# Feed-forward of a two-layer step: the up-projection by seven block products, the down-projection in a stage of its own, GpSimd adding the weight blocks

## The chip, the cores and the metric

One core of a Trainium2 chip. The metric is the device time of one launch in microseconds (us), median of several runs. TensorE (PE; PEld is its weight load), VectorE (DVE), ScalarE (ACT), GpSimd (POOL) and SyncE (SP, which issues the transfers here) each run their own list of instructions in order and wait for each other on semaphores.

## The reference, cut to what matters

A step of a model of two layers over 1088 tokens (1024 of a prompt, 64 of a sample), in float32. Each layer is an attention mixer, its output projection, and a gated feed-forward with a convolution over three tokens:

```python
def conv_ffn(h, buf, w_up, w_conv, b_conv, w_down):
    gate, up = jnp.split(h @ w_up, 2, axis=-1)
    ...
    ext = jnp.concatenate([buf.astype(gate.dtype), gate], axis=1)
    gc = b_conv + ext[:, 0:s_len] * w_conv[0]
    for i in range(1, CONV_W):
        gc = gc + ext[:, i:i + s_len] * w_conv[i]
    y = (jax.nn.silu(gc) * up) @ w_down
    return y, ext[:, ext.shape[1] - (CONV_W - 1):]
```

`h` is 1088 x 1024, `w_up` 1024 x 5632 (2816 gate features, then 2816 up features), `w_down` 2816 x 1024; there is one such pair of matrices for each layer.

## The kernel before

Every large product of float32 is made as three products of rounded parts (`three_passes`): an operand is split into a high part (ACT copies it to the rounded type) and a low part (DVE subtracts that copy from it), and high x high, high x low and low x high are summed in one PSUM bank. Each of the three is a weight load of 128 x 128 and a matmul that streams the tokens.

`output_projection` is the stage ahead of the feed-forward. It goes over nine tiles of 128 tokens: product, residual sum into `xres` (which stays in SBUF, 4.25 MB), the norm, a transposition, and the split of the normed tile into high (into the buffers `mixed`) and low parts (`hlow`).

`conv_ffn` does both products in one loop of 11 rounds (`i`). A round takes two chunks (`c`) of 128 features. Of each chunk TensorE makes the gate and the up half (`s`) in three blocks of tokens (`TB`: 384, 384, 320), each over 8 slices `k` of the 1024 inputs. ACT moves the gate block to `G` and applies the first tap; DVE applies the other two; ACT applies silu; DVE multiplies by the up half; ACT and DVE split the result into `ahi` and `alo`. Then TensorE makes the down product of the round's 256 features for nine token tiles, two halves of 512 columns each, into four PSUM banks `dn`, and DVE adds each half to `xres`. SP fetches the next chunk of `w_up` (two transfers of 512 KB) once TensorE has done with the chunk in that buffer. The order is written out by hand: each engine's list is the text of its block, and buffers and semaphores do the rest.

Stages are blocks that end for all engines together; the next begins when all have ended.

Of the kernel before, what the change touches and what calls it, by code (L numbers as in the profile page):

```python
# [12 lines left out]
ds = bass.ds  # L13
# [27 lines left out]
class Phase:  # L41
# [62 lines left out]
    def provide(nc, ctx):  # L104
# [9 lines left out]
          [f"{x}_in{s}" for x in ("q", "wkv", "raw") for s in range(2)])  # L114
# [837 lines left out]
def attention(nc, dram, consts, kind, src, home, fetch=None, soon=None):  # L952
# [17 lines left out]
    with Phase(nc, f"att_{kind}", "sync") as ph:  # L970
# [84 lines left out]
        def _(eng):  # L1055
# [489 lines left out]
def load_up(eng, dram, soon, p):  # L1545
# [7 lines left out]
def index_scores(nc, dram, consts, src, soon):  # L1553

    with Phase(nc, "index") as ph:
# [16 lines left out]
        def _(sp):  # L1572
            for p in range(2):
                load_up(sp, dram, soon, p)
                load_queries(sp, dram, soon, p)
# [214 lines left out]
def output_projection(nc, dram, consts, layer, pre, x_src, xres, mixed, hlow, nxt):  # L1790


    with Phase(nc, f"out_{layer}") as ph:
# [7 lines left out]
        norm = Norm(ph, nc, consts, lambda i: one(xres, i), dram["g_ffn"][layer])  # L1801
        mm = [ph.ps(f"mm{g}") for g in range(2)]
        taps = ph.ps("taps")
        x_in = [sem("x_in0"), sem("x_in1")]
# [3 lines left out]
        a_hi, a_lo, mm_ready, added = sem("a_hi"), sem("a_lo"), sem("mm_ready"), sem("added")  # L1808
        block = ph.block()
# [4 lines left out]
        def high_of(i):  # L1814
            return [mixed[j][1][:, :, span(i)[1]] for j in range(2)]

        def rest_of(i, rounded=0):
            q = span(i)[1]
            return [hlow[rounded][:, 0:4, q], hlow[rounded][:, 4:8, q]]

        @block.sync
        def _(sp):
            def load_x(i, slot):
                if is_last(i):
                    sp.dma_start(xres[0:DEC, NT, :], x_src[1]).then_inc(x_in[slot], 16)
                else:
                    sp.dma_start(one(xres, i), rows(x_src[0], i * P, P)).then_inc(x_in[slot], 16)

            pre.fetch(sp, FAR, raw_of[FAR], w_in)
            load_x(0, 0)  # L1830
            load_x(1, 1)
# [8 lines left out]
            with sp.Fori(0, (NT - 2) // 2) as j:  # L1840
                sp.wait_ge(x_in[0], FROM + 16 * j + 16)
                load_x(2 * j + 2, 0)
                sp.wait_ge(x_in[1], FROM + 16 * j + 16)
                load_x(2 * j + 3, 1)
            sp.wait_ge(x_in[0], FROM + 16 * (NT // 2))
            load_x(NT, 0)
            for s in range(2):
                sp.dma_start(nxt["up"][0][:, s], dram["w_up"][layer].rearrange("(k p) (s f) -> p s k f", p=P, s=2)[:, s, :, 0:P]).then_inc(
                    nxt["raw_in"], 16)

        @block.scalar
        def _(act):
# [11 lines left out]
            def high(i, slot):  # L1864

                n = span(i)[0]
                if not is_first(i):
                    act.wait_ge(mm_ready, FROM + 2 * (i - 1))
                for j in range(2):
                    s.activation(ahi[slot][:, 4 * j:4 * j + 4, 0:n], half(i, j), ACT.Copy).then_inc(a_hi, 1)  # L1870

            def keep(i):
                norm.act_square(act, i, added, 2 * i + 2)
                norm.act_root(act, i)

            def normed(i):
                act.wait_ge(a_lo, FROM + 2 * i + 2)
                norm.act_hi(act, i, high_of(i), rest_of(i))

            high(0, 0)  # L1880
            split_w(0)
            for i, slot in steps(act):
                if is_first(i):
                    split_w(1)
                else:
                    keep(i - 1)
                if not is_last(i):
                    high(i + 1, 1 - slot)
                if not is_first(i):
                    normed(i - 1)  # L1890
            keep(NT)
            s.preload_act_table_set("silu_and_others")
            normed(NT)

        @block.vector
        def _(dve):
# [9 lines left out]
            def low(i, slot):  # L1906

                n = span(i)[0]
                for j in range(2):
                    dve.wait_ge(a_hi, FROM + 2 * i + j + 1)  # L1910
                    z = ahi[slot][:, 4 * j:4 * j + 4, DEC:P] if is_last(i) else alo[slot][:, 4 * j:4 * j + 4, :]
                    v.tensor_tensor(z, half(i, j),
                                    ahi[slot][:, 4 * j:4 * j + 4, 0:n].bitcast(F32), ALU.subtract).then_inc(a_lo, 1)

            def add(i, slot):
                n = span(i)[0]
                dve.wait_ge(x_in[slot], FROM + 8 * i + (8 if slot else 16))
                for g in range(2):
                    dve.wait_ge(mm_ready, FROM + 2 * i + g + 1)
                    xs = one(xres, i)[0:n, g * 512:(g + 1) * 512]  # L1920
# [5 lines left out]
            def normed(i):  # L1926
                norm.dve_scale_g(dve, i, rest_of(i), span(i)[0])
                norm.dve_lo(dve, i, high_of(i), rest_of(i), rest_of(i, 1))

            low(0, 0)  # L1930
            split_w(0)
            dve.wait_ge(norm.g_in, FROM + 16)
            for i, slot in steps(dve):
                if is_first(i):
# [502 lines left out]
```

## Time and profile before

| what | value |
|---|---|
| median of 3 runs | 3162.0 us (3161.82 to 3163.7) |
| span of the profiled execution | 3158.3 us, 3.7 us below the median |
| PE busy | 2975.5 us, 94% of the span |
| DVE / ACT / POOL busy | 1718.0 / 1290.5 / 176.0 us |
| mean granted TensorE clock | 0.969 of 2.4 GHz |

The span runs from the first to the last instruction of the profiled execution; what the launch adds around it is the difference to the median. A busy PE counts overlapping matmuls once, and each matmul's record is longer than the distance to the next, so rates are read from the starts.

### The profile page before, as it was taken

What the parts mean: (1) busy time and instruction counts of PE and PEld (TensorE: products, weight loads), DVE (VectorE), ACT (ScalarE), POOL (GpSimd) and SP (SyncE); (2) the same over time, 40 slices, a digit from 0 to 9 for tenths busy, and PEclk for the clock granted to TensorE, in tenths of its full rate; (3) what the DMA queues carried; (4) which work ended last, traced back from release to release, by engine and by line L of the source; (5) the groups of instructions that cost most, each with busy time, mean ns of one, the idle gap of its engine ahead of it and who ended that gap; (6) DMA issues with size and microseconds to landing.
All of it is one profiled execution on the core that took longest, in us unless ns stands there. A gap on an engine that the chain in (4) does not pass through costs nothing. (4 is left out here: it accounts for less than half of the span.)

```text
span 3158.3 us, 48814 instructions
## 1 busy us (share of the span) xinstructions
PE 2975.5 (94%) x17421; PEld 2520.5 (80%) x17421; DVE 1718.0 (54%) x3696; ACT 1290.5 (41%) x2754; POOL 176.0 (6%) x240
## 2 busy tenths in 40 slices
PE   8986998998999999999899799989989999999998
PEld 6762555677999999999799567865779999999998
DVE  5438998854444455444431664169644444455445
ACT  4436995543222222222243555368532222222223
POOL 0000224400000000000000330000000000000000
PEclk9986999999999999999999899999999999999999
DMA  4110001021111111111311201110201111111111
GB/s 146 55 43 7 13 14 48 2 78 57 54 40 40 41 52 40 40 52 41 134 50 47 81 2 64 56 58 1 78 27 40 52 41 40 40 53 40 40 47 70
DMA packets 146190, 151.97 MB, mean 48 GB/s; under 512 B 17116, under 2 KB 122196, under 8 KB 146068
## 3 DMA queue, kind: packets, MB, share of 16 engines
q1 hardware_dynamic: 146068, 150.44, 15.4%
q8 instruction: 65, 1.06, 0.1%
q14 instruction: 57, 0.47, 0.0%
HBM read 126.65 MB, written 23.24 MB: 47 GB/s over the span
## 5 line engine op out<-in xcount | busy, mean ns | idle before, releaser
L247 PE MATMUL ffn_up<-hlow_r,ffn_uhi 128*128 128x384 f32 (+1 forms) x2112 | 690.8, 327 | 0.0
L2205 DVE SCALAR_TENSOR_TENSOR ffn_cv<-ffn_G,ffn_ctap,ffn_cv 128x256 f32<-128x256 f32 (+1 forms) x352 | 168.9, 501 | 492.0 <-ACT ffn_cv L2131 487.3
L2125 ACT ACTIVATE ffn_G<-ffn_up 128x384 f32<-128x384 f32 (+2 forms) x176 | 65.3, 397 | 820.9 <-PE ffn_up L248 820.9
L247 PEld LDWEIGHTS ffn_up<-hlow_r,ffn_uhi 128*128 128x128 f32 x2112 | 398.0, 188 | 0.9
L2238 DVE TENSOR_TENSOR xres<-ffn_dn,xres 128x512 f32<-128x512 f32 (+1 forms) x396 | 263.7, 687 | 132.4 <-PE ffn_dn L248 121.1
L246 PE MATMUL ffn_dn<-ffn_dhi,ffn_ahi 128*128 128x512 f32 x704 | 280.7, 399 | 2.9
L248 PE MATMUL ffn_dn<-ffn_dhi,ffn_alo 128*128 128x512 f32 x704 | 278.3, 395 | 0.0
L247 PE MATMUL ffn_dn<-ffn_dlo_r,ffn_ahi 128*128 128x512 f32 x704 | 278.3, 395 | 0.0
L246 PE MATMUL ffn_up<-mixed_c_r,ffn_uhi 128*128 128x384 f32 (+1 forms) x528 | 174.7, 331 | 4.1 <-DVE ulo_r L2182 4.1
L246 PE MATMUL ffn_up<-mixed_a_r,ffn_uhi 128*128 128x384 f32 (+1 forms) x528 | 174.6, 331 | 4.1 <-DVE ulo_r L2182 4.1
L246 PE MATMUL ffn_up<-mixed_d_r,ffn_uhi 128*128 128x384 f32 (+1 forms) x528 | 174.1, 330 | 0.0
L246 PE MATMUL ffn_up<-mixed_b_r,ffn_uhi 128*128 128x384 f32 (+1 forms) x528 | 173.8, 329 | 0.0
L246 PEld LDWEIGHTS ffn_dn<-ffn_dhi,ffn_ahi 128*128 128x128 f32 x704 | 132.2, 188 | 42.4 <-DVE xres L2238 12.5
L248 PEld LDWEIGHTS ffn_dn<-ffn_dhi,ffn_alo 128*128 128x128 f32 x704 | 132.2, 188 | 31.9
L247 PEld LDWEIGHTS ffn_dn<-ffn_dlo_r,ffn_ahi 128*128 128x128 f32 x704 | 132.3, 188 | 30.0
L2136 ACT ACTIVATE ffn_cv<-ffn_cv 128x384 f32<-128x384 f32 x132 | 67.0, 508 | 182.3 <-DVE ffn_cv L2205 182.3
L246 PE MATMUL out_mm<-out_whi,out_ahi 128*128 128x512 f32 x256 | 104.3, 407 | 7.8 <-DVE wo_odd_r L1903 4.5
L2217 DVE TENSOR_TENSOR ffn_alo<-ffn_cv,ffn_ahi 128x384 fp32r<-128x384 f32 x132 | 67.9, 514 | 77.4 <-ACT ffn_ahi L2140 77.4
L2212 DVE TENSOR_TENSOR ffn_cv<-ffn_up,ffn_cv 128x384 f32<-128x384 f32 x132 | 70.7, 536 | 69.2 <-ACT ffn_cv L2136 69.2
L2131 ACT ACTIVATE ffn_cv<-ffn_G,ffn_ctap 128x384 f32<-128x384 f32 (+2 forms) x176 | 103.6, 612 | 4.4
L246 PEld LDWEIGHTS ffn_up<-mixed_a_r,ffn_uhi 128*128 128x128 f32 x528 | 99.6, 189 | 5.0 <-DVE ulo_r L2182 4.5
L246 PEld LDWEIGHTS ffn_up<-mixed_c_r,ffn_uhi 128*128 128x128 f32 x528 | 99.6, 189 | 5.0 <-DVE ulo_r L2182 4.5
(477 smaller groups left out, 6961.2 us busy)
## 6 DMA issues: line engine op xcount, KB each, us to landing
ulo<-in_w_up_dram SPq DMA_DIRECT2D x44, 512.0 KB, 5.1
ffn_ulo<-in_w_up_dram SPq DMA_DIRECT2D x44, 512.0 KB, 4.7
ffn_dlo<-in_w_down_dram SPq DMA_DIRECT2D x22, 1024.0 KB, 4.9
w_d<-in_w_in_odd_dram SPq DMA_DIRECT2D x7, 768.0 KB, 10.4
proj_even_x<-in_x_prompt_dram SPq DMA_DIRECT2D x8, 512.0 KB, 3.3
xres<-in_x_prompt_dram SPq DMA_DIRECT2D x8, 512.0 KB, 4.4
scratch_x<-xres SPq DMA_DIRECT2D x8, 512.0 KB, 3.7
x_d<-scratch_x SPq DMA_DIRECT2D x8, 512.0 KB, 3.9
```

The source lines that it names most:

```text
L246: nc.tensor.matmul(out, lh, rh, start=first, stop=False)
L247: nc.tensor.matmul(out, lh, rl, start=False, stop=False)
L248: return nc.tensor.matmul(out, ll, rh, start=False, stop=last)
L2125: s.activation(G[:, g0:g0 + w], upbank(c, b, 0)[:, j:j + w], ACT.Copy).then_inc(g_out, 1)
L2131: last = s.activation(cv[:, 0, j:j + w], G[:, g0 - 2:g0 - 2 + w], ACT.Identity, scale=ctap[:, c, 0:1], bias=ctap[:, c, 3:4])
L2136: s.activation(cv[:, 1, 0:n], cv[:, 0, 0:n], ACT.Silu).then_inc(silu_done, 1)
L2205: last = v.scalar_tensor_tensor(cv[:, 0, j:j + w], G[:, g0 - 2 + tapno:g0 - 2 + tapno + w], ctap[:, c, tapno:tapno + 1], cv[:, 0, j:j + w] ...
L2212: v.tensor_tensor(cv[:, 1, 0:n0], upbank(c, b, 1)[:, 0:n0], cv[:, 1, 0:n0], ALU.mult).then_inc(a_done, 1)
L2217: last = v.tensor_tensor(to, cv[:, 1, c0 - t0:c1 - t0], ahi[:, c, c0:c1].bitcast(F32), ALU.subtract)
L2238: v.tensor_tensor(xs, dn[j % 4][0:n, :], xs, ALU.add).then_inc(half_added if t == NT else dn_added, 1)
```

## The change

`output_projection` no longer keeps `xres`: tiles of the residual stream go through a ring of four buffers `xb`, are stored to a DRAM scratch (`att`) after the sum, and the normed tile stays whole in float32 (in `mixed`). For the second half of the tokens DVE forms three sums of quarter blocks there (`fold`). The first chunk of `w_up` is fetched, summed (on DVE) and split in this stage too.

`conv_up` is a new stage. A round `m` (22 of them) makes 128 gate and the 128 matching up features for all tokens. The inputs are halved (`hT[0]`, `hT[1]`: 4 slices each) and the tokens are halved (2 x 544); the 2 x 2 by 2 x 2 block product is made from seven products (`p1` to `p7`) of sums of blocks, as Strassen's scheme in Winograd's form does. Each product goes over 4 slices and two quarters `s` of 272 tokens. Partial sums stay in two PSUM banks x and y for each quarter, two rounds deep; ACT copies and DVE adds them out between the products, and TensorE adds further products on top of what a bank still holds. Seven weight blocks (slots of `low`, `high`) are needed, four as loaded or overwritten and three sums; `add_up` makes them with four operations of 128 x 512 on GpSimd, for the round to come. The result `U` of a round is stored to a DRAM scratch (`a`).

`conv_down` is a new stage as well: it fetches weights, the features of two rounds and (first) the whole residual stream back from DRAM, three buffers deep, splits both operands and makes the same down products as before into eight PSUM banks. `far`/`late` fetches of the next stage's weights are all issued in it.

```diff
+PRODUCTS = ("p1", "p2", "p6", "p5", "p7", "p3", "p4")
+BATCHES = ((0, 2), (4, 7), (2, 4))
+def add_up(v, eng, raw, sums, before):
+    v.tensor_tensor(raw[:, 4], raw[:, 2], raw[:, 3], ALU.add).then_inc(sums, 1)
+    v.tensor_tensor(raw[:, 2], raw[:, 0], raw[:, 2], ALU.subtract).then_inc(sums, 1)
+    eng.wait_ge(sums, FROM + before + 1)
+    v.tensor_tensor(raw[:, 5], raw[:, 4], raw[:, 0], ALU.subtract).then_inc(sums, 1)
+    eng.wait_ge(sums, FROM + before + 3)
+    v.tensor_tensor(raw[:, 6], raw[:, 1], raw[:, 5], ALU.subtract).then_inc(sums, 1)
+def act_high(nc, act, raw, high, sums, hi, before, batches=range(3)):
+    for b in batches:
+        if b:
+            act.wait_ge(sums, FROM + before + 4)
+        j0, j1 = BATCHES[b]
+        nc.scalar.activation(high[:, j0:j1], raw[:, j0:j1], ACT.Copy).then_inc(hi, 1)
...
+def conv_up(nc, dram, consts, layer, hT, first):
...
+            for m in range(1, NF):
+                if m >= 2:
+                    sp.wait_ge(up_ready, ready(m - 2, "p4", 1))
+                load_up(sp, dram, layer, m, low[m % 2], raw_in[m % 2])
+                if m >= 2:
+                    sp.wait_ge(a_done, FROM + m - 1)
+                    sp.dma_start(dram["a"][m - 2], U[m % 2][:]).then_inc(a_out[m % 2], 16)
...
+            for m in range(1, NF):
+                first_tap(m - 1)
+                copy(m, "c11")
+                silu(m - 1)
+                copy(m, "c12")
+                weights(m + 1, (0, 1))
+                copy(m, "c22")
+                weights(m + 1, (2,))
+                copy(m, "c21")
...
+            for m in range(1, NF):
+                taps(m - 1)
+                keep_tail(m - 1)
+                set_seam(m)
+                add(m, "c11")
+                gated(m - 1)
+                weights(m + 1, (0,))
+                add(m, "c22")
+                weights(m + 1, (1,))
+                add(m, "c12")
+                weights(m + 1, (2,))
...
+        @block.gpsimd
+        def _(pool):
+            for m in range(1, NF):
+                pool.wait_ge(raw_in[m % 2], FROM + 32 * ((m + 1) // 2))
+                add_up(nc.gpsimd, pool, low[m % 2][0], sums, 4 * prepared(m))
...
+                        if what in ("p6", "p7", "p3"):
+                            pe.wait_ge(taken, taken_of(m, {"p6": "c11", "p7": "c12", "p3": "c22"}[what], s))
+                        if what in ("p5", "p4"):
+                            pe.wait_ge(added, added_of(m, {"p5": "c11", "p4": "c22"}[what], s))
+                        if m == 0:
+                            pe.wait_ge(t_lo, FROM + 2 * PRODUCTS.index(what) + s + 1)
+                        j = SLOT[what]
+                        for k in range(4):
+                            last = three_passes(nc, bank[:, 0:QUARTER], (high[m % 2][:, j, k, :], low[m % 2][1][:, j, k, :]),
+                                                (moving_high(what, s)[:, k, :], spot(what, s, 1)[:, k, :]),
+                                                what in ("p1", "p2", "p5") and k == 0, k == 3, True)
...
+def conv_down(nc, dram, consts, layer, first, out, x_next, fetch):
...
+        ring = 3
+        xres = sb("xres", [P, TILES, D])
...
+        dn = [ph.ps(f"dn{j}") for j in range(8)]
...
+            def load(i):
+                s = i % ring
+                sp.dma_start(w[s][0][:], wdn[i * 2 * P:(i + 1) * 2 * P].rearrange("(c p) n -> p c n", p=P)).then_inc(w_in[s], 16)
+                for j in range(2):
+                    sp.wait_ge(a_out[j], FROM + 16 * (i + 1))
+                sp.dma_start(a[s][0][:], dram["a"][2 * i:2 * i + 2].rearrange("c p n -> p c n")).then_inc(a_in[s], 16)
```

**ACT, in the loop of the up product.** Before, the second chunk of a round in the middle of the loop: `ffn_G` is the gate block, `ulo` the next chunk of weights.

```order
L2125 ACTIVATE ffn_G<-ffn_up 128x384
L2131 ACTIVATE ffn_cv<-ffn_G,ffn_ctap 128x384
L2136 ACTIVATE ffn_cv<-ffn_cv 128x384
L2140 ACTIVATE ffn_ahi<-ffn_cv 128x384
L2108 ACTIVATE ffn_uhi<-ulo 128x1024 x2
L2125 ACTIVATE ffn_G<-ffn_up 128x384
L2131 ACTIVATE ffn_cv<-ffn_G,ffn_ctap 128x384
L2136 ACTIVATE ffn_cv<-ffn_cv 128x384
```

Of the change, one round of `conv_up`: taps of the round before, then copies out of the banks x and y, and between them the high parts of the next round's weights (`high`).

```order
L2147 ACTIVATE up_cv<-up_G,tap 128x1024
L2147 ACTIVATE up_cv<-up_G,tap 128x64
L2133 ACTIVATE up_G<-up_x 128x272 x2
L2153 ACTIVATE up_cv<-up_cv 128x1088
L2133 ACTIVATE up_G<-up_x 128x272
L2133 ACTIVATE up_G<-up_x 128x208
L2133 ACTIVATE up_G<-up_x 128x64
L1824 ACTIVATE high<-low 128x1024
L1824 ACTIVATE high<-low 128x1536
L2138 ACTIVATE up_U<-up_y 128x272 x2
L1824 ACTIVATE high<-low 128x1024
L2138 ACTIVATE up_U<-up_x 128x272 x2
```

The rounding of the weights moved from between two token blocks to between two copies that TensorE's products wait for, and its second piece (128x1536) needs the sums from GpSimd.

**SP, from the up product to the down product.** Before, the head of `conv_ffn` and the first rows of its loop: `ffn_ulo` and `ulo` are chunks of `w_up`, `ffn_dlo` the rows of `w_down`, `wc_soon` the next stage's weights.

```order
L2044 DMA ffn_ulo<-in_w_up_dram 128x8x128 x2
L2047 DMA ffn_dlo<-in_w_down_dram 128x2x1024
L287 DMA wc_soon<-in_w_in_odd_dram 128x1544 x3
L2053 UNCONDITIONAL_BRANCH
L2053 ISA
L2044 ISA
L2044 DMA ulo<-in_w_up_dram 128x8x128
```

Of the change, the end of `conv_up` and the head of `conv_down` (numbers are buffers): `scratch_a` holds the features, `dn_0_alo` and `dn_0_wlo` are the operands of the down product before they are split, `scratch_att` and `dn_0_xres` the residual stream.

```order
L2118 DMA scratch_a<-up_0_U0 128x1088
L2118 DMA scratch_a<-up_0_U1 128x1088
L57 UNCONDITIONAL_BRANCH
L2331 UNCONDITIONAL_BRANCH
L2335 DMA dn_0_wlo0<-in_w_down_dram 128x2x1024
L2338 DMA dn_0_alo0<-scratch_a 128x2x1088
L2345 DMA dn_0_xres<-scratch_att 128x3x1024
L2335 DMA dn_0_wlo1<-in_w_down_dram 128x2x1024
L2338 DMA dn_0_alo1<-scratch_a 128x2x1088
```

Before, the features never left SBUF, and the weights of a round's down product were fetched beside its up product; now the last features are stored, a stage ends, and weights and features are fetched at the head of the next, with the residual stream between them.

## Rows read from the trace of the kernel before

**Rows 1.** Busy time by stage: output projection, feed-forward of layer 0, of layer 1.

```profile
core 0: us, PE busy (x) PEld busy (x) DVE busy (x) ACT busy (x) POOL busy (x), PEclk, DMA share, GB/s
646.50:762.60 116.10, 107.77 (x490) 87.61 (x490) 63.90 (x110) 42.25 (x80) 0.00 (x0) 0.96 0.19 53
762.60:1561.20 798.60, 794.66 (x4312) 738.95 (x4313) 384.31 (x691) 215.73 (x364) 0.00 (x0) 1.00 0.17 54
...
2349.00:3148.00 799.00, 795.00 (x4312) 739.33 (x4313) 391.78 (x704) 226.57 (x386) 0.00 (x0) 1.00 0.15 47
```

**Rows 2.** Waits in layer 0's feed-forward: who for whom, total us, times, longest.

```profile
PEld ffn_dn L246 <- DVE xres L2238: 6.3, 11, 0.6
```

**Rows 3.** Timeline of PE, first and last of three runs of matmuls: start us, length.

```profile
849.73 0.33 PE L247 MATMUL ffn_up<-hlow_r,ffn_uhi 128*128 128x384 f32 x1
...
855.63 0.33 PE L248 MATMUL ffn_up<-mixed_b_r,ulo_r 128*128 128x384 f32 x1
855.80 0.31 PE L246 MATMUL ffn_up<-mixed_a_r,ffn_uhi 128*128 128x320 f32 x1
...
861.95 0.31 PE L246 MATMUL ffn_up<-mixed_b_r,ffn_uhi 128*128 128x320 f32 x1
...
1554.65 0.40 PE L246 MATMUL ffn_dn<-ffn_dhi,ffn_ahi 128*128 128x512 f32 x1
...
1559.54 0.40 PE L254 MATMUL ffn_dn<-ffn_dhi,ffn_ahi 128*128 128x512 f32 x1
```

**Rows 4.** Timeline, eight weight loads of a transposition of 128 columns, in sequence.

```profile
667.88 1.02 PEld L220 LDWEIGHTS out_ht<-ident,out_hn 128*128 128x128 f32 x8
```

**Rows 5.** ACT by shape in layer 0's feed-forward: busy us, mean ns, idle before.

```profile
L2131 ACT ACTIVATE ffn_cv<-ffn_G,ffn_ctap 128x384 f32<-128x384 f32 x44 | 31.2, 710 | 1.5
L2108 ACT ACTIVATE ffn_uhi<-ffn_ulo 128x1024 fp32r<-128x1024 f32 x22 | 22.1, 1053 | 19.6 <-DMA ffn_ulo<-in_w_up_dram 19.6
L2112 ACT ACTIVATE ffn_dhi<-ffn_dlo 128x2048 fp32r<-128x2048 f32 x11 | 20.9, 1901 | 0.0
L2125 ACT ACTIVATE ffn_G<-ffn_up 128x256 f32<-128x256 f32 x22 | 8.5, 385 | 61.2 <-PE ffn_up L248 61.2
```

**Rows 6.** DVE by shape, output projection and feed-forward of layer 0.

```profile
L2238 DVE TENSOR_TENSOR xres<-ffn_dn,xres 128x512 f32<-128x512 f32 x176 | 117.1, 688 | 64.9 <-PE ffn_dn L248 64.5
L2205 DVE SCALAR_TENSOR_TENSOR ffn_cv<-ffn_G,ffn_ctap,ffn_cv 128x384 f32<-128x384 f32 x88 | 54.5, 619 | 164.0 <-ACT ffn_cv L2131 162.4
L2182 DVE TENSOR_TENSOR ulo_r<-ulo,ffn_uhi 128x1024 fp32r<-128x1024 f32 x22 | 26.0, 1222 | 5.0 <-ACT ffn_uhi L2108 5.0
L2187 DVE TENSOR_TENSOR ffn_dlo_r<-ffn_dlo,ffn_dhi 128x2048 fp32r<-128x2048 f32 x11 | 25.2, 2292 | 13.7 <-ACT ffn_dhi L2112 13.7
```

**Rows 7.** POOL by shape, whole span: one input and a scalar, three attention stages.

```profile
L1087 POOL TENSOR_SCALAR att_c_prob<-att_c_prob,att_c_rr 128x1024 f32<-128x1024 f32 x8 | 9.0, 1121 | 14.4 <-DVE att_c_rr L1364 14.4
...
L1087 POOL TENSOR_SCALAR att_a_prob<-att_a_prob,att_a_rr 128x512 f32<-128x512 f32 x8 | 7.8, 980 | 6.5 <-DVE att_a_rr L1364 6.3
...
L1087 POOL TENSOR_SCALAR att_c_prob<-att_c_prob,att_c_rr 128x512 f32<-128x512 f32 x8 | 5.5, 692 | 7.1 <-DVE att_c_rr L1364 7.1
```

**Rows 8.** Timeline, from the output projection into layer 0's feed-forward.

```profile
761.93 0.42 DVE L240 TENSOR_TENSOR hlow_r<-hlow,mixed_b_r 128x256 fp32r<-128x256 f32 x1 [0.15 <-ACT mixed_b_r L235]
762.63 0.99 SPq L2044 DMA_DIRECT2D ffn_ulo<-in_w_up_dram  x2
...
765.11 0.69 PE L246 MATMUL ffn_up<-mixed_a_r,ffn_uhi 128*128 128x384 f32 x1 [4.12 <-DVE ulo_r L2182]
...
768.44 2.01 ACT L2108 ACTIVATE ffn_uhi<-ffn_ulo 128x1024 fp32r<-128x1024 f32 x2 [3.77 <-DMA ffn_ulo<-in_w_up_dram]
```

**Rows 9.** Two stretches behind that start, columns as in the first group.

```profile
765.10:769.00 3.90, 3.90 (x13) 3.90 (x14) 1.09 (x1) 0.56 (x1) 0.00 (x0) 0.52 1.10 342
769.00:775.00 6.00, 6.00 (x36) 6.00 (x35) 2.61 (x4) 1.45 (x2) 0.00 (x0) 1.00 1.02 417
```

**Rows 10.** DMA issues by line, whole span: count, KB each, median us to landing.

```profile
ffn_dlo<-in_w_down_dram SPq DMA_DIRECT2D x22, 1024.0 KB, 4.9
```

More of the change, by code:

```diff
@@ L1800, in output_projection @@
         rowbuf = sb("rowbuf", [P, 2 * P])
-        norm = Norm(ph, nc, consts, lambda i: one(xres, i), dram["g_ffn"][layer])
+        xb = [sb(f"x{s}", [P, D]) for s in range(RING)]
+        norm = Norm(ph, nc, consts, lambda i: xb[i % RING][:], dram["g_ffn"][layer])
         mm = [ph.ps(f"mm{g}") for g in range(2)]
         taps = ph.ps("taps")
-        x_in = [sem("x_in0"), sem("x_in1")]
+        x_in, x_mid = [[sem(f"{x}{s}") for s in range(2)] for x in ("x_in", "x_mid")]
         w_in, w_hi, w_lo = sem("w_in"), sem("w_hi"), sem("w_lo")
@@ L1974, in _, with quarter @@
                     norm.pe_transposes(pe, i - 1)
-                multiply(i, slot, 1)
+                multiply(i, 1)
             norm.pe_transposes(pe, NT)
-def one_col(m):
-    return slice(m, m + 1) if isinstance(m, int) else ds(m, 1)
-TB = [(0, 384), (384, 384), (768, 320)]
 CW = 2 + SEQ + 2 + DEC
+SEAM = 2 + SEQ
 NG = NF // 2
-def conv_ffn(nc, dram, consts, layer, xres, hT, first, out, x_next, fetch):
-    wup, wdn = dram["w_up"][layer], dram["w_down"][layer]
+def quarter(s, half):
+    return half * HALF + s * QUARTER
@@ new lines, in _ @@
+            sp.wait_ge(tail_out, FROM + 1)
+            for g, name in ((0, "p_conv"), (1, "s_conv")):
+                for j in range(2):
+                    r0 = (2 * g + j) * NF
+                    sp.dma_start(out[name][layer, j].rearrange("(c p) -> c p", p=P), rowbuf[r0:r0 + NF, 0:P]).then_inc(state_out, 16)
+            for i in range(ring, NG):
+                sp.wait_ge(dn_ready, FROM + 18 * (i - ring + 1))
+                load(i)
+                if i == 4 and fetch is not None:
+                    fetch.fetch_soon(sp)
@@ L2076, in _ @@
                     sp.dma_start(to, xres[0:n, t, :]).then_inc(x_out[t % 2], 16)
-            sp.wait_ge(tail_out, FROM + 1)
-            for g, name in ((0, "p_conv"), (1, "s_conv")):
-                for j in range(2):
-                    r0 = (2 * g + j) * NF
-                    sp.dma_start(out[name][layer, j].rearrange("(c p) -> c p", p=P), rowbuf[r0:r0 + NF, 0:P]).then_inc(state_out, 16)
             for s in range(2):
@@ L2154, in _ @@
+            s_ = nc.scalar
+            for i in range(NG):
+                s = i % ring
+                act.wait_ge(w_in[s], FROM + 16 * (i // ring + 1))
+                s_.activation(whi[s][:], w[s][0][:], ACT.Copy).then_inc(hi, 1)
+                act.wait_ge(a_in[s], FROM + 16 * (i // ring + 1))
+                s_.activation(ahi[s][:, :, 0:TOK], a[s][0][:], ACT.Copy).then_inc(hi, 1)
+            s_.preload_act_table_set("sqrt_and_others")
             if last_layer:
@@ L2241, in _ @@
                         xs = xres[0:n, t, g * 512:(g + 1) * 512]
-                        v.tensor_tensor(xs, dn[g][DEC:P, :], xs, ALU.add).then_inc(dn_added, 1)
-                    if last_layer and not more and t:
+                        v.tensor_tensor(xs, dn[(18 * i + 2 * t + g) % 8][DEC:P, :], xs, ALU.add).then_inc(dn_added, 1)
+                    if last_layer and i == NG - 1 and t:
                         if t == 1:
```

638 lines of the change are left out of this document (363 added, 275 removed).

## The prediction, made before the changed kernel was timed

> **What bounds the kernel now.** I read the busy time by stage first [rows 1]. The two feed-forwards take 798.6 and 799.0 us, half of the span, and TensorE is busy in all but 4 us of each; DVE and ACT are busy in half and in a quarter. The waits [rows 2] name the only repeated one on TensorE: its down product waits for DVE 11 times in a layer, 6.3 us in all. So the stage is as long as TensorE's list, and the next view is the spacing of matmuls in the timeline [rows 3]: 34 steps of 384 tokens in 5.90 us, 173.5 ns each; 42 steps of 320 tokens in 6.15 us, 146.4 ns; 21 steps of 512 columns in 4.89 us, 232.9 ns. A chunk of the up product is 96 matmuls of 384 and 48 of 320: 23.68 us. A round's down product is 104 of 512: 24.2 us. 22 chunks and 11 rounds make 787.4 us; with the 6.3 us, the start (2.5 us from the stage's first transfer to the first matmul [rows 8]) and a slow beginning (below) that is the 798.6.
>
> **The up product.** A round is now 7 x 2 x 4 x 3 = 168 matmuls of 272 tokens instead of 144 longer ones. The trace has no such length. From 320 to 384 each column costs 0.423 ns, so I take 146.4 - 48 x 0.423 = 126.1 ns. Lower bound: the 384 row scaled by columns, 122.9 ns. Upper bound: no shorter than 320 tokens, 146.4 ns. A floor from the weight loads, one for each matmul as before, does not bind: the eight of a transposition follow each other every (1.02 - 0.19) / 7 = 119 ns, 0.19 being the length of one [rows 4]. A round is then 21.18 us (20.6 to 24.6), 2.50 less, and 44 rounds give **-110 us** (-134 to +40).
>
> **Waits inside a round.** Set t = 0 where p1 begins; a product takes 3.03 us, and they begin at 0, 3.0, 6.1, 9.1, 12.1, 15.1 (p3) and 18.2 (p4). Prices: ACT copies 272 columns in 0.40 us (385 ns for 256), rounds 1024 in 1.05 and 1536 in 1.48 (halfway from 1053 to 1901) [rows 5]; DVE needs 1.22 for 1024 and, by its slope of 1.045 ns per column, 1.29 for 1088, 1.76 for 1536 and some 0.44 for 272 [rows 6]. DVE's list of a round comes to 11 us, ACT's to 10, so neither is the bound; order decides. ACT copies the last of p4 by 0.6, applies the first tap by 2.2, copies p1's sums by 3.7, applies silu by 6.4 and copies p6's by 9.9. Then it rounds slots 0 and 1 (to 10.9) and **waits for all four sums** before slots 4 to 6; behind that wait stands the copy of p5's sums, and p3 on TensorE waits for that copy. With 1.48 + 0.40 + 0.1 to go, the sums must be there at 13.1.
>
> GpSimd starts when the next chunk has landed. SP asks for it when p4 ends (0.3), and two such transfers were in use 5.8 us after the request [rows 8]: t = 6.1. (The store of `U` stands behind it in SP's queue, waits for DVE until about 8, and is out of the way before the next request.) An add of two inputs of 128 x 512 on GpSimd isn't in the trace. Its one-input form takes 692 ns, 263 of it fixed by the step from 512 to 1024 columns, 980 in another stage [rows 7]. Bounds: 0.69 us, and twice 0.98 = 1.96 us. I take 1.25, between a doubled streaming part (263 + 2 x 429 = 1.12) and a doubled whole (1.38). Four with a semaphore between end at 6.1 + 5.2 = 11.3: 1.8 us to spare. But the same row at 692 and 980 ns says that GpSimd is sometimes held up, and DVE's product `gated` (1.29, ready at 6.7) and its first low part (1.22, ready at 11.0) fall into that stretch; if both go first the sums are ready at 13.8, 0.7 late. I take 0.3 us for each of the 2 x 20 rounds that prepare a next one this way: **+12 us** (0 to 28 at that price, 140 at 1.96 us with both holds: 16.6, 3.5 late).
>
> The Trainium skill speaks against this move: GPSIMD Engine Reference, section 3.1 (Elementwise), gives 4497 ns for a two-input add of 2048 columns against 2293 on VectorE and advises VectorE. A quarter is an estimate of 1.12 us, with which the sums are 0.2 late if both holds occur and in time otherwise. DVE does 512 columns in 688 ns [rows 6], yet DVE isn't what the round waits for, so the dearer engine costs nothing until 13.1.
>
> **Between the stages.** Up and down no longer overlap. After the last matmul of the up product: copy 0.4, first tap over 1088 columns 1.6 (710 ns for 384, plus 0.83 per further column, and a second piece) [rows 5], two taps on DVE at 1.5 (619 ns for 384) [rows 6], silu 1.1, product 1.3: 7.6 us. Store issued and stage ended: 8.6 (from the end of one stage's last work, 762.35, to the next one's first transfer is 0.3 [rows 8]). 1 MB of `w_down` lands 4.9 us after its issue [rows 10]: 13.5. ACT rounds it in 1.9 [rows 5]; the features, 1.1 MB behind it in the queue, have landed by 15 at 417 GB/s [rows 9]; rounding them (2176 columns) ends at 17.4, and DVE's low part (2.3 and a small piece) at 20.1. TensorE starts at 20.5. After an idle time it is slow at first: for the 3.9 us behind the start at 765.1 its granted clock was 0.52, the 1.2 GHz level, and 13 matmuls began where 22 would have [rows 9]: 9 x 0.1735 = 1.6 us lost. That start exists before the change too; the second one in a layer is new. So 22.1 us for each layer, **+44 us** (36, without the wait for a second transfer, to 58, with twice the landing time). The 4.3 MB of residual stream come in between: all of the 10.8 MB first asked for land at 8.6 + 1 + 26 = 36 at 417 GB/s, and DVE needs the last tiles at 20.5 + 12 x 1.4 = 37. At 342 GB/s they come at 41; eight banks hold 11 us of products, so TensorE still doesn't wait. I count 0.
>
> **The down product** keeps its 104 matmuls a round. Its wait for DVE goes, as eight banks replace four and DVE's list (20 sums of 0.69, two low parts: 18.7 us) fits into 24.2: **-12.6 us** (-12.6 to 0).
>
> **The output projection.** Two roundings on ACT and two low parts on DVE go from each tile. In come, on DVE, sums and low part of the first chunk (four of 0.69; 4.2 us) and, for five tiles, `fold`: four of 0.69 us behind a tile's sum and ahead of the next norm. Most hides under the 11 us of TensorE's tile. At the end the last two folds (2.75 and 1.7) lie on the path, the roundings (about 1) and ACT's norm beside the first don't add: +2; two tiles where the norm comes about 1 us late: +2. **+8 us** for both layers (0 to 16). The first round of `conv_up` splits the seven token blocks itself: DVE's 14 low parts of 1.29 us run ahead of TensorE's 1.51 a quarter, so its start stays at about 2.5 us; **+2**.
>
> **Sum:** -110 + 12 + 44 - 12.6 + 8 + 2 = -56.6; 3158.3 - 56.6 = 3101.7 in the span, and with the 3.7 us that the median lies above it 3105.
>
> **Rivals.** *GpSimd and DVE hold each other up for whole instructions.* The sums then end at 13.8 to 14.4 (adds of 1.25 to 1.4), 0.7 to 1.3 late: 28 to 52 us for the 40 rounds instead of 12, 3121 to 3145. For it speaks the 980 against 692 ns; against it, that these two rows differ by 0.29 us only. By the Trainium skill, SBUF — State Buffer, section Who interferes with whom, a VectorE instruction with two SBUF inputs and a GpSimd instruction that reads SBUF exclude each other for a whole instruction. No run here shows it for two-input adds yet.
>
> *GpSimd becomes the bound (slower than before).* Everything but this term is -68.6 us, 1.7 for each of 40 rounds: from sums at 14.8 on the kernel loses. That is an add of 2.1 us without holds or 1.5 us with both. At 1.96 with both it is 3162 - 68.6 + 140 = 3233; at 1.6 with both, 2.1 late, 3177. Behind the late sums, p3 on TensorE would wait in every round.
>
> *Short matmuls aren't shorter in proportion.* At 132 ns the up product gives -66 instead of -110: 3149. Against it: the 119 ns of transpositions.
>
> *All waits hidden, and the gap at its lower bound:* 3162 - 110 + 36 - 12.6 + 4 = 3079, with 4 for the last two terms.
>
> **How the numbers follow.** Forecast as summed, 3085 to 3122: 0.5. Holds, 3122 to 3148: 0.2. GpSimd the bound, 3155 to 3235: 0.12. Matmuls of 130 ns and more, 3130 to 3165: 0.08. Better than 3085: 0.1. The range of 8 in 10 is 3080 to 3160. A measurement can tell about 0.2%, 6 us, from no change. Faster by more than that: 0.83; within: 0.03; slower: 0.14.
>
> **What would show it.** Steps of 126 ns between matmuls of 272 tokens, 21.2 us a round; GpSimd's adds at 1.25 us, four ending before 13.1; no idle time of TensorE ahead of p3 (or 0.3 us, put down to ACT's copy from y); some 20 us without matmuls between the up and down stage, and granted clock near 0.5 for 4 us behind it; no waits for DVE in the down stage. The prediction is wrong if TensorE idles ahead of p3 by over a microsecond, if 272 tokens take over 130 ns, or if the gap is nearer 35 than 22.

## The result, and the profile after

The changed kernel takes 3072.2 us (median of 4 runs, 3070.51 to 3074.93), the kernel before 3161.9 in the same series: a ratio of 0.9719, 95% interval 0.9705 to 0.9733. It is faster by 89.7 us, where the forecast was 57; 3072 lies 8 us below the lower end of the range. The profiled execution has a span of 3068.7 us.

Busy time by stage, with the columns of [rows 1]: output projection, up and down stage of layer 0, then of layer 1.

```profile
645.75:764.08 118.33, 107.93 (x490) 87.72 (x490) 69.49 (x119) 34.96 (x65) 0.00 (x0) 0.95 0.26 90
764.08:1242.73 478.65, 466.67 (x3696) 466.23 (x3696) 269.39 (x409) 206.13 (x341) 130.82 (x84) 0.99 0.23 72
1242.73:1522.65 279.92, 262.42 (x1145) 216.60 (x1145) 197.09 (x254) 44.66 (x23) 0.00 (x0) 0.96 0.37 141
2188.46:2306.84 118.38, 107.97 (x490) 87.73 (x490) 69.58 (x119) 34.96 (x65) 0.00 (x0) 0.95 0.26 90
2306.84:2784.40 477.56, 466.68 (x3696) 466.24 (x3696) 265.09 (x409) 206.01 (x341) 129.64 (x84) 0.99 0.23 72
2784.40:3068.70 284.30, 262.90 (x1145) 216.91 (x1145) 208.63 (x272) 57.66 (x50) 0.00 (x0) 0.96 0.32 120
```

TensorE has work in all but some 30 us of a feed-forward. The rate is in the spacing; timeline of PE, first and last of 169 steps of 272 tokens and of 107 steps of 512 columns (columns as in [rows 3]):

```profile
899.77 0.29 PE L249 MATMUL up_x<-up_th,low_r 128*128 128x272 f32 x1
...
920.97 0.29 PE L247 MATMUL up_x<-up_th,up_high 128*128 128x272 f32 x1
...
1399.66 0.39 PE L249 MATMUL dn_dn<-dn_whi,dn_alo_r 128*128 128x512 f32 x1
...
1423.91 0.39 PE L249 MATMUL dn_dn<-dn_whi,dn_alo_r 128*128 128x512 f32 x1
```

That is 125.4 ns a step in the up product (forecast 126.1), and 226.6 ns in the down product, where [rows 3] had 232.9 for the same length. SP's fetches give the length of whole rounds, since each waits for the end of a product. Timeline of SP, kernel before, a round of `conv_ffn`:

```profile
983.95 0.37 SPq L2047 DMA_DIRECT2D ffn_dlo<-in_w_down_dram  x1
1007.76 1.00 SPq L2044 DMA_DIRECT2D ulo<-in_w_up_dram  x2
1031.54 1.00 SPq L2044 DMA_DIRECT2D ffn_ulo<-in_w_up_dram  x2
1056.18 0.37 SPq L2047 DMA_DIRECT2D ffn_dlo<-in_w_down_dram  x1
```

The same of the changed kernel, one round of `conv_up` and one of `conv_down` from fetch to fetch:

```profile
855.31 1.00 SPq L1804 DMA_DIRECT2D up_low<-in_w_up_dram  x2
...
876.39 0.99 SPq L1804 DMA_DIRECT2D low<-in_w_up_dram  x2
...
1305.11 0.37 SPq L2335 DMA_DIRECT2D dn_wlo<-in_w_down_dram  x1
...
1328.68 0.38 SPq L2335 DMA_DIRECT2D dn_wlo<-in_w_down_dram  x1
```

A round of the kernel before is 72.23 us: two chunks of 23.79 and a down product of 24.64. Now a chunk is 21.07 (21.07 or 21.08 from one fetch to the next), which is 168 x 125.4 ns, and the down product is 23.57, which is 104 x 226.6 ns. Whether waits hide in these spacings, the view of TensorE's waits tells (its products in layer 0, up stage, then down stage):

```profile
PE up_x L247 <- DVE mixed_a_r L2237: 4.8, 1, 4.8
PE up_y L247 <- DVE up_G L2205: 1.3, 1, 1.3
PE dn_dn L247 <- DVE dn_alo_r L2425: 12.0, 1, 12.0
```

Each is a single wait (4.8 and 12.0 at the start of a stage, 1.3 in the first round), so no wait is left in the rounds that repeat.

How GpSimd's adds went: timeline of the changed kernel, one round, with what bears on p3 (in brackets: idle time before, and who ended it).

```profile
1192.29 0.29 PE L247 MATMUL up_x<-up_th,high 128*128 128x272 f32 x1
...
1198.74 1.28 POOL L1810 TENSOR_TENSOR up_low<-up_low 128x512 f32<-128x512 f32 x1 [15.23 <-DMA up_low<-in_w_up_dram]
1198.85 2.33 DVE L2232 TENSOR_TENSOR up_U<-up_cv,up_U 128x1088 f32<-128x1088 f32 x1
...
1199.99 2.34 POOL L1811 TENSOR_TENSOR up_low<-up_low 128x512 f32<-128x512 f32 x1
...
1202.30 1.29 POOL L1813 TENSOR_TENSOR up_low<-up_low 128x512 f32<-128x512 f32 x1
...
1203.66 1.29 POOL L1815 TENSOR_TENSOR up_low<-up_low 128x512 f32<-128x512 f32 x1
...
1204.98 1.49 ACT L1824 ACTIVATE up_high<-up_low 128x1536 fp32r<-128x1536 f32 x1 [2.06 <-POOL up_low L1815]
...
1206.37 0.67 ACT L2138 ACTIVATE up_U<-up_y 128x272 f32<-128x272 f32 x2
...
1207.34 0.29 PE L247 MATMUL up_y<-up_th,high 128*128 128x272 f32 x1
```

p1 begins at 1192.29, so t = 0 is there. The adds begin at t = 6.45 and end at 12.66; p3 begins at 15.05, with no idle time ahead of it. ACT waits 2.06 us for the sums, but the copy behind them ends in time. This is the latest of layer 0's 20 rounds with adds: in the others they begin at 5.8 to 6.3 and end at 12.0 to 12.5 (in layer 1 at 12.9 at the latest). An add takes 1.28 us alone. The second takes 2.34: it starts at 1199.99, and DVE's product `gated` (1.28 us when alone, below) runs to 1201.18. `gated` took 2.33, having itself stood still until the first add ended.

Between the stages, timeline of the changed kernel in layer 0: last matmul up, first fetch down, the roundings, first matmul down.

```profile
1234.31 0.29 PE L249 MATMUL up_x<-up_th,up_low_r 128*128 128x272 f32 x1
...
1242.73 0.38 SPq L2335 DMA_DIRECT2D dn_wlo<-in_w_down_dram  x1
...
1247.91 1.91 ACT L2385 ACTIVATE dn_whi<-dn_wlo 128x2048 fp32r<-128x2048 f32 x1 [7.25 <-DMA dn_wlo<-in_w_down_dram]
1250.63 2.02 ACT L2387 ACTIVATE dn_ahi<-dn_alo 128x2176 fp32r<-128x2176 f32 x1 [0.81 <-DMA dn_alo<-scratch_a]
...
1252.89 2.28 DVE L2425 TENSOR_TENSOR dn_alo_r<-dn_alo,dn_ahi 128x2048 fp32r<-128x2048 f32 x1
...
1255.23 0.79 PE L247 MATMUL dn_dn<-dn_whi,dn_ahi 128*128 128x512 f32 x1 [12.04 <-DVE dn_alo_r L2425]
```

The gap is 20.6 us (forecast 20.5) and holds one short matmul alone, for the convolution's tail. For 4 us behind it the granted clock is 0.50, the 1.2 GHz level, with 9 matmuls where 18 would have begun:

```profile
1255.20:1259.20 4.00, 3.97 (x9) 3.13 (x10) 0.86 (x2) 1.91 (x1) 0.00 (x0) 0.50 1.02 410
```

The balance of both layers, in the order of the forecast's sum (stages by their first transfers; what is left of a feed-forward besides whole rounds is "gap and starts"):

| term | forecast | measured | from |
|---|---|---|---|
| up product | -110 | -119.7 | 44 x (21.07 - 23.79) |
| p3 waits for sums | +12 | 0 | 21.07 = 168 x 0.1254 |
| gap and starts | +46 | +49.3 | 25.0 and 24.3 |
| down product | -12.6 | -23.5 | 22 x (23.57 - 24.64) |
| output projection | +8 | +4.1 | 118.3 and 118.4 for 116.1 and 116.5 |
| elsewhere | 0 | +0.4 | |
| sum | -56.6 | -89.4 | spans: 3158.3 - 3068.7 = 89.6; the 0.2 is rounding |

### The profile page after: what moved, and what is told of

It is laid out like the page before. It is cut to its first block and busy times, and to the rows that moved or that the text cites. A ratio compares the mean times of both kernels' runs of the same rounds, so it can differ in the third digit from the quotient of the medians.

```text
span 3068.7 us, 48809 instructions
## 1 busy us (share of the span) xinstructions
PE 2841.1 (93%) x18477; PEld 2407.0 (78%) x18477; DVE 1884.6 (61%) x3650; ACT 1346.4 (44%) x2724; POOL 436.5 (14%) x408
## 5 line engine op out<-in xcount | busy, mean ns | idle before, releaser
L2445 DVE TENSOR_TENSOR dn_xres<-dn_dn,dn_xres 128x512 f32<-128x512 f32 (+1 forms) x396 | 266.8, 688 | 135.2 <-PE dn_dn L249 125.0
L247 PE MATMUL dn_dn<-dn_whi,dn_ahi 128*128 128x512 f32 x704 | 276.3, 393 | 24.2 <-DVE dn_alo_r L2425 24.2
L248 PE MATMUL dn_dn<-dn_wlo_r,dn_ahi 128*128 128x512 f32 x704 | 276.0, 392 | 0.0
L249 PE MATMUL dn_dn<-dn_whi,dn_alo_r 128*128 128x512 f32 x704 | 275.7, 392 | 0.0
L247 PE MATMUL up_x<-up_th,high 128*128 128x272 f32 x704 | 205.3, 292 | 9.7 <-DVE mixed_a_r L2237 4.8
L249 PE MATMUL up_x<-up_th,low_r 128*128 128x272 f32 x704 | 205.9, 292 | 0.0
L249 PE MATMUL up_x<-up_th,up_low_r 128*128 128x272 f32 x704 | 203.7, 289 | 0.0
L247 PE MATMUL up_x<-up_th,up_high 128*128 128x272 f32 x704 | 202.7, 288 | 0.0
L247 PE MATMUL up_y<-up_th,high 128*128 128x272 f32 x528 | 152.2, 288 | 1.6 <-DVE up_G L2205 1.6
L247 PE MATMUL up_y<-up_th,up_high 128*128 128x272 f32 x528 | 151.9, 288 | 0.0
## 6 DMA issues: line engine op xcount, KB each, us to landing
dn_xres<-scratch_att SPq DMA_DIRECT2D x4, 1536.0 KB, 14.4
```

What stands on the lines that cost most here:

```text
L247: nc.tensor.matmul(out, lh, rh, start=first, stop=False, skip_group_check=on_top)
L248: nc.tensor.matmul(out, lh, rl, start=False, stop=False, skip_group_check=on_top)
L249: return nc.tensor.matmul(out, ll, rh, start=False, stop=last, skip_group_check=on_top)
L2445: v.tensor_tensor(xs, bank[0:n, :], xs, ALU.add).then_inc(half_added if t == NT else dn_added, 1)
```

## Experiments

Ratios are to the kernel before, timed beside each; the changed kernel's is 0.9719.

### What GpSimd's adds cost

**sums_on_dve.** The four sums back on DVE (`weight_sums` waits for the chunk and calls `add_up` with DVE):

```diff
                 gated(m - 1)
+                weight_sums(m + 1)
                 weights(m + 1, (0,))
-        @block.gpsimd
...
-                add_up(nc.gpsimd, pool, low[m % 2][0], sums, 4 * prepared(m))
```

> The changed kernel, with the four sums of the weight blocks back on DVE (behind its product of the gated features) in conv_up. My theory: in the changed kernel the sums end at t = 12.7 of a round (GpSimd starts at 6.45, three adds of 1.3 us and one that waits 1.2 us for a DVE product), 0.4 us before the deadline 13.1, so GpSimd's adds cost TensorE nothing; DVE has some 10 us a round to spare and needs 4 x 0.69 = 2.8 us, done by about 10.5. Both are hidden: the period of a round stays 21.07 us and the time stays within 6 us of the changed kernel's 3072. Rival A, that GpSimd's adds do cost something by holding DVE up: faster by more than 6 us. Rival B, that DVE is nearer to its limit than its list says and its sums push the reads of the banks back: TensorE waits for DVE's additions ahead of p5 or p4, 0.5 us in 40 rounds would be 20 us, 3092.

Measured: 3071.6 us, 0.9714 (0.9700 to 0.9727): the same. Timeline, DVE in one round:

```profile
1199.12 1.28 DVE L2232 TENSOR_TENSOR up_U<-up_cv,up_U 128x1088 f32<-128x1088 f32 x1
1200.32 0.68 DVE L1810 TENSOR_TENSOR up_low<-up_low 128x512 f32<-128x512 f32 x1
...
1202.24 0.69 DVE L1815 TENSOR_TENSOR up_low<-up_low 128x512 f32<-128x512 f32 x1
```

`gated` is back at 1.28 us, the sums are done 2 us earlier, and neither is on TensorE's path. That GpSimd makes them is worth nothing here and costs nothing that the intervals (some 4 us either way) could show.

**pool_two_more.** Two adds more on GpSimd in each round:

```diff
+                nc.gpsimd.tensor_tensor(raw[:, 6], raw[:, 0], raw[:, 1], ALU.add)
+                nc.gpsimd.tensor_tensor(raw[:, 5], raw[:, 0], raw[:, 3], ALU.add)
                 add_up(nc.gpsimd, pool, raw, sums, 4 * prepared(m))
```

> The changed kernel, with two more adds of 128x512 on GpSimd ahead of the four in each round of conv_up; their results are overwritten by the sums. My theory: the sums then end 2 x 1.3 = 2.6 us later, at t = 15.3 instead of 12.7, 2.2 us behind the deadline of 13.1; TensorE idles ahead of p3 in each of 40 rounds, 1.6 to 2.2 us each, 64 to 88 us, put down to ACT's copy out of a bank y: 3136 to 3160. Rival, that p3 isn't what ends last (the deadline lies later, or the round has slack in p4): under 30 us more, below 3102.

Measured: 3146.6 us, 0.9952 (0.9937 to 0.9968). View of the waits of TensorE:

```profile
PE up_y L247 <- ACT up_U L2138: 59.1, 40, 2.7
```

40 waits ahead of p3, put down to ACT's copy, as the forecast described them; most rounds take 22.6 to 22.8 us instead of 21.07. The sums end at t = 14.8 in the round of the timeline (14.6 to 15.3 in all but the first of layer 0); there p3 begins 1.85 us behind its sums, so to begin at 15.05 it needs them at 13.2 (forecast 13.1). The deadline is real, and the changed kernel keeps it by half a microsecond in the round shown, by about one in most and by 0.3 us in the closest.

### Why the down product is shorter

**down_four_banks.** Four PSUM banks instead of eight:

```diff
-                        if j >= 8:
-                            pe.wait_ge(dn_added, FROM + j - 7)
+                        if j >= 4:
+                            pe.wait_ge(dn_added, FROM + j - 3)
...
-                        bank = dn[(18 * i + j) % 8]
+                        bank = dn[(18 * i + j) % 4]
```

> The changed kernel, with four PSUM banks instead of eight in conv_down. Two things differ between the down product before and after: 22 waits of 0.57 us for DVE are gone, and the 512-column matmuls begin every 226.6 ns instead of every 232.9 ns. Theory: the number of banks explains the waits alone. Then the waits come back, up to 12.6 us in all, and the spacing stays at 226.6: 3072 to 3085. Rival: the number of banks also sets the spacing (TensorE writes to a bank beside one that DVE reads): 232.9 ns, another 14 us, 3098.

Measured: 3070.3 us, 0.9717 (0.9704 to 0.9731); 226.7 ns. In the view of the waits the only one of the down product for DVE is that of each stage's start:

```profile
PE dn_dn L247 <- DVE dn_alo_r L2425: 25.1, 2, 13.0
```

So the number of banks explains neither the waits nor the spacing: the waits of [rows 2] don't come back. Timeline of DVE in the kernel before, where a down product begins at 1536.77 and the first sum could have run from about 1538.3, when its six matmuls were through:

```profile
1541.43 0.42 DVE L2217 TENSOR_TENSOR ffn_alo<-ffn_cv,ffn_ahi 128x256 fp32r<-128x256 f32 x1 [0.54 <-ACT ffn_ahi L2140]
1541.77 0.22 DVE L2217 TENSOR_TENSOR ffn_ahi<-ffn_cv,ffn_ahi 128x64 fp32r<-128x64 f32 x1
1541.91 3.13 DVE L2238 TENSOR_TENSOR xres<-ffn_dn,xres 128x512 f32<-128x512 f32 x5
```

DVE still had the last token block of the up product in hand. In the parted stage four banks are enough, so the wait went because the stages were parted.

**before_pe_unrolled.** The kernel before, without TensorE's loop:

```diff
-            with pe.Fori(0, NG) as i:
+            for i in range(NG):
```

> The kernel before, with TensorE's list of conv_ffn written out 11 times instead of a loop; nothing else. Theory: the 512-column matmuls of the down product begin every 232.9 ns before and every 226.6 ns after because of the loop (the changed kernel has none); here they come down to 226.6, 22 x 104 x 6.3 ns = 14 us, 3148. Rival: the spacing goes with where the operands lie or what reads them, not with the loop: 232.9 stays and the time is within 4 us of 3162.

Measured: 3164.8 us, 1.0011 (1.0002 to 1.0020); 77 steps of 512 columns in 17.96 us, 233.2 ns. Not the loop.

**before_shift32, after_shift32.** 32 bytes ahead of the operands of the down product, in either kernel:

```diff
+        sb("gap", [P, 8])
         dhi = sb("dhi", [P, 2, D], F32R)        # before; in conv_down ahead of xres
```

> The kernel before, with a gap of 32 bytes ahead of the buffer of the high part of the down weights, so that this and all buffers behind it in the stage move by 32 bytes (moving operand of the down product from 0 to 32 modulo 64, stationary one from 32 to 0). The 512-column matmuls of the down product begin every 232.9 ns before and every 226.6 ns after, and neither the loop nor the number of banks explains it. Theory: the place of the operands does; the spacing comes to 226.6 to 230, 3147 to 3155. Rival: it does not, 232.9 and 3161.

> The changed kernel, with a gap of 32 bytes ahead of all buffers of conv_down (moving and stationary operands from 32 to 0 modulo 64). Theory, that the place of the operands sets the spacing of the 512-column matmuls: it leaves 226.6 ns and comes to 230 to 233, 3080 to 3086. Rival: it stays at 226.6 and the time at 3072.

Measured: 3160.4 us (0.9998, 0.9989 to 1.0008) with 233.2 ns, and 3071.7 us (0.9718, 0.9703 to 0.9733) with 226.6 ns. Both as they were: where each operand lies modulo 64, taken by itself, doesn't set it.

**down_places.** In layer 1, the buffers of round 0, 3, ... at the places of the kernel before, those of the other rounds at places far apart (`w`, `whi`: moving operand; `a`, `ahi`: stationary):

```diff
+            w = [two(f"wlo{s}", [P, 2, D], (131264, 173216, 81952)[s]) for s in range(ring)]
+            whi = [put(f"whi{s}", [P, 2, D], F32R, (123072, 165024, 73760)[s]) for s in range(ring)]
+            a = [two(f"alo{s}", [P, 2, TOK], (156128, 65056, 190624)[s]) for s in range(ring)]
+            ahi = [put(f"ahi{s}", [P, 2, SEQ + P], F32R, (146912, 55840, 181408)[s]) for s in range(ring)]
```

> The changed kernel, with the buffers of the down product of layer 1 (not of layer 0) at fixed places: those of rounds 0, 3, 6, 9 at the very places that the kernel before used for them, those of rounds 1, 4, 7, 10 with the moving operand high and the stationary one low in SBUF, those of rounds 2, 5, 8 the other way round. Theory, that the place sets the spacing of the 512-column matmuls: 232.9 ns in rounds 0, 3, 6, 9 (0.65 us more for such a round than for one of layer 0), and perhaps another figure in one of the other two groups. Rival: 226.6 ns in all rounds, as in layer 0, and the cause lies elsewhere.

Measured (one run): 3078.5 us. Timeline of SP, one round of layer 0, then of layer 1:

```profile
1423.00 0.37 SPq L2344 DMA_DIRECT2D dn_wlo<-in_w_down_dram  x1
...
1446.58 0.37 SPq L2344 DMA_DIRECT2D dn_wlo<-in_w_down_dram  x1
...
2849.70 0.37 SPq L2344 DMA_DIRECT2D at_wlo<-in_w_down_dram  x1
...
2873.97 0.37 SPq L2344 DMA_DIRECT2D at_wlo<-in_w_down_dram  x1
```

23.58 us in layer 0, 24.27 in layer 1, and there in all three groups of rounds (24.15 to 24.27). The place matters, but not as either side had it: all three pairs are slow. What they share is that moving and stationary operand differ modulo 256 bytes (192 and 224; 160 and 32; 32 and 160), while the fast runs have them equal (32 and 32; 64 and 64, by the places of the buffers in the programs).

**before_in_step, after_apart_288, after_apart_256.** That guess, put to both kernels:

```diff
+        sb("gap", [P, 56])                       # before: 224 bytes ahead of ahi and alo
         ahi = sb("ahi", [P, 2, NT * P + P], F32R)
...
+        sb("gap", [P, 72])                       # after: 288 (or 256: [P, 64]) ahead of the features
         a = [ph.twin(f"alo{s}", [P, 2, TOK]) for s in range(ring)]
```

> The kernel before, with a gap of 224 bytes ahead of the features' high part, so that moving and stationary operands of the down product lie at the same place modulo 512 bytes (192; before: 192 and 480). Theory, from the runs so far: the 512-column matmuls begin every 226.6 ns when both operands lie at the same place modulo 512 (32 and 32 in the changed kernel, 64 and 64 in the run shifted by 32 bytes) and every 233 ns when they don't (192 and 480 before, 224 and 0 in the shifted one, and 160 and 32, 32 and 160 in the run with fixed places). Then here 226.6 ns, 14 us less: 3147. Rival, that something else about the places sets it (how high in SBUF a buffer lies): 233 ns and 3161.

> The changed kernel, with a gap of 288 bytes between the weights and the features of conv_down (moving operand at 32, stationary one at 320 modulo 512, the distance that they have in the kernel before). Theory, same place modulo 512: 233 ns a matmul, 22 x 104 x 6.3 = 14 us more, 3086. Rival: 226.6 ns and 3072.

> The same with a gap of 256 bytes (32 and 288 modulo 512). If the rule goes by 256 bytes the spacing stays 226.6 ns, 3072; if by 512 it is 233 ns, 3086.

Timelines of PE, first and last matmul: `before_in_step`, 78 steps, 226.9 ns:

```profile
1537.26 0.40 PE L247 MATMUL ffn_dn<-ffn_dlo_r,ffn_ahi 128*128 128x512 f32 x1
...
1554.96 0.39 PE L255 MATMUL ffn_dn<-ffn_dlo_r,ffn_ahi 128*128 128x512 f32 x1
```

and `after_apart_288`, 104 steps, 233.4 ns:

```profile
1449.68 0.40 PE L248 MATMUL dn_dn<-dn_wlo_r,dn_ahi 128*128 128x512 f32 x1
...
1473.95 0.40 PE L248 MATMUL dn_dn<-dn_wlo_r,dn_ahi 128*128 128x512 f32 x1
```

Measured: 3152.3 us (0.9967, 0.9954 to 0.9979), 3088.4 us (0.9754, 0.9738 to 0.9771) and, for 256 bytes, 3072.5 us in one run with 226.6 ns. So 224 bytes make the kernel before faster, 288 cost the changed one 16 us, and 256 nothing: it goes by 256 bytes. (The changed kernel says the same of 512: the second half of its low features lies 4352 bytes behind the first, which is 17 x 256, and all its matmuls have the short spacing.) The kernel before gains about 10 us rather than 14; its wait for DVE takes back 1.4 in each layer, as TensorE reaches it sooner (view of the waits, layer 0; 6.3 us in [rows 2]):

```profile
PEld ffn_dn L246 <- DVE xres L2239: 7.7, 11, 0.7
```

### What the gap is worth

**down_ahead.** The first round's weights and features fetched and split in the last round of `conv_up`, which has no next weights to split:

```diff
+                if m == NF - 1:                  # ACT, behind the copies of p6 and p5
+                    s_.activation(ahead["whi"][:], ahead["w"][0][:], ACT.Copy).then_inc(ahead_hi, 1)
...
+                    s_.activation(ahead["ahi"][:, :, 0:TOK], ahead["a"][0][:], ACT.Copy).then_inc(ahead_hi, 1)
...
-            load(0)
```

> The changed kernel, with the weights and features of the first round of conv_down fetched and split in the last round of conv_up, in the place of the split of a next round's weights, which that round hasn't got (the buffers are those of round 20, and 9 KB that lay free). My theory: of the 20.6 us without matmuls between the two stages of a layer only the tail of conv_up (about 8.4 us to the end of the stage) is left; TensorE starts some 12 us earlier in each layer, 24 us in all: 3048. Rival A: the residual stream, or the second round's operands behind it in the queue, then come too late, and TensorE gives some of it back behind its first eight banks: 3055 to 3065. Rival B: the split in the last round delays its copies out of the banks, so that the stage ends later: about 3060.

Measured: 3047.6 us, 0.9641 (0.9628 to 0.9654). Timeline of PE between the stages:

```profile
1237.09 0.29 PE L249 MATMUL up_x<-up_th,up_low_r 128*128 128x272 f32 x1
1245.57 0.41 PE L2480 MATMUL dn_dn<-ident,tail 128*88 128x128 f32 x1 [8.19 <-PEq L57]
1245.64 0.78 PE L247 MATMUL dn_dn<-whi_ahead,up_ahi_ahead 128*128 128x512 f32 x1
```

8.3 us without products instead of 20.6, and the 24.6 us less are twice that difference: nothing came back behind it.

**ahead_in_step.** The same, with the operands of round 0 and the fetched weights of the output projection in step as well:

```diff
+            tensor(far, "step_far", [P, 48], side="right")
             mixed_a = twin(nc, far, "mixed_a", [P, 4, TOK], side="right")
```

> The kernel with the first round of the down product prepared in conv_up, and now all operands of the down product and of the output projection at the same place modulo 256 bytes (in that kernel the features' high part of round 0 and the fetched part of the output projection's weights lie at 96 and 224, the rest at 32). If the rule of the place holds for other products too, the 512-column matmuls of the output projection come from 230.3 to 226.6 ns (some 400 in a stage, 1.5 us for each layer) and round 0 of the down product from 233.3 to 226.6 (0.7 us for each layer): 4 us less than 3047.6, 3043. If it is peculiar to the down product, only 1.4 us less, 3046.

Measured: 3046.5 us, 0.9639 (0.9626 to 0.9652). Timeline of PE in the output projection, first and last of 38 steps:

```profile
694.14 0.39 PE L248 MATMUL out_mm<-wo_even_r,out_ahi 128*128 128x512 f32 x1
...
702.77 0.39 PE L247 MATMUL out_mm<-out_whi,out_ahi 128*128 128x512 f32 x1
```

227.1 ns, where 44 steps in the same stretch of the changed kernel take 230.0: in a second product the spacing falls when all operands are in step. The 230.0 is a mixture, since only the low part of the fetched weights lay apart there, about a third of the matmuls; it is half the way from 226.7 to 233, so the cost of a matmul with operands apart isn't simply the 6.3 ns of the down product. The span is 3044.8 for 3049.4 us, but the intervals of the two ratios overlap, so the times themselves don't tell the two versions apart. Both beat the changed kernel by some 25 us.

## Why the prediction was right and wrong

Right were the direction and the frame: TensorE's list sets the time, the matmul of 272 tokens is shorter in proportion, and the parted stages cost about 20 us and a slow clock for each layer. The gap's parts came as worked out, from the stage's end to the first matmul (12.5 us, forecast 11.9), with 9 matmuls in 4 us behind it. Of the rivals, the short matmuls and GpSimd as the bound are out; "all waits hidden" (3079) was nearest, but by luck: it took the gap at its lower bound (36), and the gap and starts came to 49.3. None of the three signs that the prediction named for being wrong appeared; it missed on the side for which it had named none.

The 33 us between the sum and the measurement lie in four steps, all on the same side.

**The down product, 11 us.** "The down product keeps its 104 matmuls a round" was right, and the step that failed is what was taken with it, unsaid: that each keeps its 232.9 ns. The operands moved to other buffers, and the spacing fell to 226.6: 22 x 104 x 6.3 ns = 14.4 us. `before_in_step` and `after_apart_288` show it in both directions. Beside that the wait is worth 9.1 us of the 23.5, or 13.5 where the spacing goes first (`before_in_step` gains 10), against 12.6 forecast: its size was about right, half of its reason was not. "Eight banks replace four" changes nothing (`down_four_banks`); DVE no longer comes late from the up product.

**Waits inside a round, 12 us.** The step that failed is "if both go first", with 0.3 us a round taken between "to spare" and "late" without a row for it. Only `gated` can stand in GpSimd's way: DVE's first low part waits for the four sums themselves. The changed kernel, cut:

```diff
+def dve_low(nc, dve, low, high, sums, hi, lo, j, batches=range(3)):
+    for b in batches:
+        if b == 0:
+            dve.wait_ge(sums, FROM + 4 * j + 4)
...
```

One hold of 1.1 us and adds of 1.29 instead of 1.25 end at 12.66, between the 11.3 and 13.8 of the forecast and ahead of the deadline, so not even the 0.3 us occur. `pool_two_more` shows that the deadline and the price were right. The rival "hold each other up for whole instructions" is true in its mechanism (2.34 and 2.33 us), and free.

The Trainium skill, SBUF — State Buffer, section Who interferes with whom, states that exclusion for a VectorE instruction with two SBUF inputs and a GpSimd instruction that reads SBUF; the trace agrees. By the Trainium skill, GPSIMD Engine Reference, section 3.1 (Elementwise), a quarter of its add of 2048 columns is an estimate of 1.12 us; the trace has 1.28, and `sums_on_dve` shows that the dearer engine indeed cost nothing.

**The up product, 10 us.** Half is the spacing, 125.4 for 126.1 ns (4.8 us). Half is the kernel before: the rows at 849.73 gave 23.68 us a chunk, while two fetches 23.78 and 23.81 apart show 23.79 (4.8 us). One stretch of 34 steps stood for all; the length of a whole round was there to be read.

**The output projection, 4 us:** +4.1 instead of +8. Perhaps more of `fold` lies under TensorE's tiles than was counted; no run took this apart, so the step that failed stays open here. Against these, the gap and the starts cost 3.3 us more, and the rest of the program 0.4.

## What to carry to other kernels

Where a term is "unchanged", ask whether the instruction still reads the same buffers; read a rate from the length of whole rounds rather than from one stretch. Where the two operands of long matmuls lie in SBUF is worth a look: 224 bytes of padding alone took 10 us from the kernel before. A cost on an engine beside the bound counts only past its deadline, so work out which instructions can stand in its way at all: one that waits for the result cannot. A stage that begins with a fetch and a split can have both done in the last round of the stage before, where the work for a next round is missing.

## What the runs showed of the hardware

In the down products of both kernels the matmul of 512 fp32r columns with its own weight load begins every 226.6 to 227.1 ns when moving and stationary operand lie at the same place modulo 256 bytes in SBUF (differences of 0 and 256 bytes were run), and every 232.2 to 233.4 ns when they don't (32 and 128 modulo 256). In the output projection putting all operands in step took 230.0 ns to 227.1. For 272 columns the runs don't tell: rows of 544 inputs (2176 bytes) and quarters of 272 (1088 bytes) put most moving operands of each of the seven products elsewhere modulo 256 than their weights, and no run moved them. Why the place matters, and what happens at other lengths, stays open.

A GpSimd add and a DVE operation, each with two inputs in SBUF, took turns by whole instructions: 2.34 us for 1.28 and 2.33 for 1.28.
